# Attention's outputs turned by VectorE in 32x32 squares instead of by TensorE, with gates and results moved by squares

## What is computed

```python
h = rms_norm(x, norm_pre) * (1.0 + scale) + shift      # shift, scale, gate from silu(c) @ ada_w + ada_b
q, k, v, z = h @ w_in                                   # 4 x 2048 columns
p = softmax(mask(q k^T * scale)) for both halves m      # mask: key chunk <= query chunk
attn = p[:, :, 0] - lam * p[:, :, 1]
o = attn @ v                                            # per head, 256 wide
o = rms_norm(o, subln_g) * (1.0 - lambda_init)          # over the head's 256 values
o = o * silu(z)
x = x + gate * rms_norm(o @ w_out, norm_post)
```

## Time and profile before

| | |
|---|---|
| median of 3 runs | 1907.08 us (1906.72 to 1908.92) |
| the profiled execution | 1907.34 us |
| its span, first to last instruction | 1905.5 us |
| mean granted TensorE clock | 0.999 |

### The profile page before, as it was taken

The page is one execution under the profiler, slowest core; times in us unless marked ns, Lnnn a source line. Parts: engine busy times, 40 slices in busy tenths (PEclk is TensorE's granted clock), DMA queues, the critical chain, the costliest instruction groups (busy, mean ns, idle before and its releaser), DMA issues.

```text
span 1905.5 us, 26384 instructions
## 1 busy us (share of the span) xinstructions
PE 1866.0 (98%) x9072; PEld 1540.9 (81%) x9072; DVE 1379.5 (72%) x2028; ACT 810.1 (43%) x1516; POOL 794.4 (42%) x844
## 2 busy tenths in 40 slices
PE   4999999999999999999999999999999999999998
PEld 1488888888888888888888888888888888888886
DVE  3687888886655546787887877878778776569467
ACT  5633333333444433444443444444444445546452
POOL 2076565655644523344344434434443422116023
PEclk9999999999999999999999999999999999999999
DMA  9898898886674698786877778686777679657777
GB/s 354 253 313 279 274 297 278 284 290 232 214 267 160 237 356 263 225 250 192 253 229 227 235 216 252 198 254 212 232 240 221 213 228 291 207 186 257 258 240 265
DMA packets 394048, 473.16 MB, mean 248 GB/s; under 512 B 22614, under 2 KB 268476, under 8 KB 391228
## 3 DMA queue, kind: packets, MB, share of 16 engines
q1 hardware_dynamic: 393632, 471.43, 76.4%
q10 hardware_dynamic: 284, 0.05, 0.0%
HBM read 323.54 MB, written 147.86 MB: 247 GB/s over the span
## 4 chain that ended last, share of the span: by engine, by line
PE 93%; DVE 1%; DMA 1%; ACT 0%; issue 0%; SPq 0%; POOL 0%; DVEq 0%; POOLq 0%; ACTq 0%
PE ps L1752 30%; PE ps L1754 30%; PE ps L1753 30%; PE ps L1885 2%; PE ps L1861 1%; PE ps L1904 1%; PE ps L1721 0%; DMA ubf<-s_dr 0%; DMA z_dr<-cc 0%; PE ps L1833 0%; DVE ring L1310 0%; ACT h L1040 0%; DVE xt L1632 0%; DVE tB L1330 0%; DVE tB L1327 0%
## 5 line engine op out<-in xcount | busy, mean ns | idle before, releaser
L1752 PE MATMUL ps<-blk,ring 128*128 128x512 f32 x1524 | 603.3, 396 | 2.6 <-DVE blk L1357 1.9
L1754 PE MATMUL ps<-blk,ring 128*128 128x512 f32 x1524 | 594.6, 390 | 0.0
L1753 PE MATMUL ps<-blk,ring 128*128 128x512 f32 x1524 | 594.2, 390 | 0.0
L1752 PEld LDWEIGHTS ps<-blk,ring 128*128 128x128 f32 x1524 | 286.3, 188 | 66.0 <-issue 9.7
L1754 PEld LDWEIGHTS ps<-blk,ring 128*128 128x128 f32 x1524 | 286.0, 188 | 60.8
L1753 PEld LDWEIGHTS ps<-blk,ring 128*128 128x128 f32 x1524 | 286.5, 188 | 55.8
L1310 DVE TENSOR_TENSOR ring<-sums,ring 128x512 fp32r<-128x512 f32 x256 | 234.7, 917 | 95.5 <-ACT ring L1006 93.6
L836 POOL TENSOR_TENSOR sums<-raw 128x512 f32<-128x512 f32 x128 | 191.5, 1496 | 226.9 <-DVE ring L1310 206.0
L1006 ACT ACTIVATE ring<-sums 128x512 fp32r<-128x512 f32 x256 | 160.6, 628 | 179.3 <-PE ps L1754 175.6
L1310 DVE TENSOR_TENSOR ring<-raw,ring 128x512 fp32r<-128x512 f32 x192 | 179.2, 934 | 58.9 <-ACT ring L1006 58.5
L836 POOL TENSOR_TENSOR sums<-sums,raw 128x512 f32<-128x512 f32 x128 | 190.2, 1486 | 20.8 <-DVE ring L1310 14.3
(11 more groups left out here) (159 smaller groups left out, 3181.7 us busy)
## 6 DMA issues: line engine op xcount, KB each, us to landing
raw<-in_diff_w_in_dram SPq DMA_DIRECT2D x64, 1024.0 KB, 7.8
d_dr<-cc SPq DMA_DIRECT2D x124, 256.0 KB, 3.2
cc<-d_dr SPq DMA_DIRECT2D x124, 256.0 KB, 4.1
ubf<-s_dr SPq DMA_DIRECT2D x113, 256.0 KB, 5.0
ada<-in_ada_w_dram SPq DMA_DIRECT2D x88, 256.0 KB, 7.3
tb<-in_diff_w_out_dram SPq DMA_DIRECT2D x32, 512.0 KB, 5.5
t_dr<-tb SPq DMA_DIRECT2D x32, 512.0 KB, 4.9
ada<-in_ada_w_dram SPq DMA_DIRECT2D x32, 512.0 KB
```

The lines of the kernel that those rows point to most:

```text
L1752: MM(dst, a_hi, b_hi, start=start, stop=False, skip_group_check=True)
L1753: MM(dst, a_hi, b_lo, start=False, stop=False, skip_group_check=True)
L1754: return MM(dst, a_lo, b_hi, start=False, stop=stop, skip_group_check=True)
```

## The change

The transposition of each block's result by TensorE goes. VectorE turns the 128x256 tile within squares of 32x32 (`V.transpose`, from SBUF into the same PSUM columns); the squares themselves stay where they are. So the gate must be loaded in that arrangement of squares, and the results are stored by squares so that `s_dr` holds what it held before: each load of z and each store becomes four DMAs of 32 partitions with runs of 32 elements (128 B) in place of one DMA of 128 partitions with runs of 512 B. The norm weight, which was a value per partition after the turn, is now a row across columns (`sub_row`, one broadcast load of 128 KB, scaled once) and is multiplied in `out_scale`. `gate` becomes a transpose and one multiplication of 128x256. The layout of `s_dr` changes so that a unit's read still has 2 KB runs.

```diff
@@ load_z
-                sp.dma_start(z_sb[:, :, :],
-                             z_dr[h * 2:h * 2 + 2, :, qb * P:(qb + 1) * P].rearrange("m p n -> p m n")).then_inc(z_ld, 16)
+                for c in range(0, P, SIDE):
+                    sp.dma_start(z_sb[c:c + SIDE].rearrange("j m (b i) -> j (m b) i", i=SIDE),
+                                 z_dr[h * 2:h * 2 + 2, :, qb * P + c:qb * P + c + SIDE].rearrange(
+                                     "m (b j) i -> j (m b) i", j=SIDE)).then_inc(z_ld, 16)
@@ store_pair
                 sp.wait_ge(ozf_ok, h * NB + 2 * p + 2)
-                sp.dma_start(s_dr[0:4, h, :, p].rearrange("o p n -> p o n"),
-                             ozf.rearrange("p i m n -> p (i m) n")).then_inc(s_st, 16)
+                for c in range(0, P, SIDE):
+                    sp.dma_start(s_dr[h, 0:4 * P, p, c:c + SIDE].rearrange("(o j) i -> j o i", j=SIDE),
+                                 ozf[c:c + SIDE].rearrange("j t m (b i) -> j (t m b) i", i=SIDE)).then_inc(s_st, 16)
                 sp.wait_ge(osum_ok, 4 * (h * PAIRS + p + 1))
-                sp.dma_start(s_dr[4:8, h, :, p].rearrange("o p n -> p o n"), osum[:, :, :]).then_inc(s_st, 16)
+                for c in range(0, P, SIDE):
+                    sp.dma_start(s_dr[h, 4 * P:8 * P, p, c:c + SIDE].rearrange("(o j) i -> j o i", j=SIDE),
+                                 osum[c:c + SIDE].rearrange("j o (b i) -> j (o b) i", i=SIDE)).then_inc(s_st, 16)
@@ load_unit
-                sp.dma_start(ubf[k][:, 1, 1], s_dr[s, h].rearrange("p t n -> p (t n)")).then_inc(unit_in[k], 16)
+                sp.dma_start(ubf[k][:, 1, 1], s_dr[h, s * P:(s + 1) * P].rearrange("p t n -> p (t n)")).then_inc(unit_in[k], 16)
@@ SP, second half of the projection
+                if n == NA + 12:
+                    sp.dma_start(sub_row[:, :], subln[None, :].to_broadcast([P, VD])).then_inc(sub_in, 16)
@@ out_scale, gate (VectorE)
-                V.tensor_scalar(o_sb[:, :], ps[:, OB, 0:VD], ofac[:, 0:1], None, ALU.mult).then_inc(o_ok, 1)
+                else:
+                    dve.wait_ge(cols_ok, 2)
+                STT(o_sb[:, :], ps[:, OB, 0:VD], ofac[:, 0:1], sub_row[:, :], ALU.mult, ALU.mult).then_inc(o_ok, 1)
@@
+                dve.wait_ge(o_ok, a + 1)
+                V.transpose(ps[:, OB, VD:2 * VD], o_sb[:, :]).then_inc(oT_done, 1)
+                dve.wait_ge(z_ld, (a + 1) * 16 * (P // SIDE))
+                if a > 1:
+                    dve.wait_ge(s_st, PAIR_STORED * (a // 2))
                 dve.wait_ge(oT_done, a + 1)
-                dve.wait_ge(z_ld, (a + 1) * 16)
-                if a > 1:
-                    dve.wait_ge(s_st, 32 * (a // 2))
-                for m in range(2):
-                    i = STT(ozf[:, a % 2, m], ps[:, OB, VD + m * P:VD + (m + 1) * P], sub8[:, m:m + 1],
-                            z_sb[:, m], ALU.mult, ALU.mult)
-                i.then_inc(ozf_ok, 1)
+                TTV(ozf[:, a % 2], ps[:, OB, VD:2 * VD].rearrange("p (m n) -> p m n", m=2), z_sb[:, :, :],
+                    ALU.mult).then_inc(ozf_ok, 1)
@@ VectorE, once
+            dve.wait_ge(sub_in, 16)
+            V.tensor_scalar(sub_row[:, :], sub_row[:, :], (1.0 - LAMBDA_INIT) / 2, None, ALU.mult).then_inc(cols_ok, 1)
@@ TensorE (and its three calls)
-            def o_turn(h, qb):
-                a = h * NB + qb
-                pe.wait_ge(o_ok, a + 1)
-                for m in range(2):
-                    last = TR(ps[:, OB, VD + m * P:VD + (m + 1) * P], o_sb[:, m * P:(m + 1) * P], ident[:, :])
-                last.then_inc(oT_done, 1)
```

More of the change, by code:

```diff
@@ L16 @@
 CHUNK = 64
+SIDE = 32
 def build(nc, x, c, ada_w, ada_b, norm_pre, norm_post, w_in, w_out, lq1, lk1, lq2, lk2, subln, out):
@@ L150, in build @@
         gpT = at("gpT", [P, P], F32)
-        sub8 = at("sub8", [P, 2], F32)
         lamp = at("lamp", [P, 2], F32)
@@ L232, in build @@
         ofac = at("ofac", [P, 1], F32, z_at)
+        sub_row = at("sub_row", [P, VD], F32, z_at)
         BLK = 2 * KB * HALF * 4
@@ L267, in build @@
         t_dr = dram("t_dr", [2, HEADS, 4, P, HALF])
-        s_dr = dram("s_dr", [8, HEADS, P, PAIRS, P])
+        s_dr = dram("s_dr", [HEADS, 8 * P, PAIRS, P])
         gp_dr = dram("gp_dr", [KT, P])
@@ L280, in build @@
         lam_p, lam_mm, lam_e, lam_ok = sem("lam_p"), sem("lam_mm"), sem("lam_e"), sem("lam_ok")
-        c_e, c_ok = sem("c_e"), sem("c_ok")
+        c_ok, sub_in = sem("c_ok"), sem("sub_in")
         x_sq, x_ss, x_ms, x_rs, x_sc = sem("x_sq"), sem("x_ss"), sem("x_ms"), sem("x_rs"), sem("x_sc")
@@ L370, in turned @@
             return a // NB * (NB + HT) + qb + max(qb - HT, 0) + half + 1
+        PAIR_STORED = 2 * 16 * (P // SIDE)
         def taken(s):
@@ L713, in load_unit @@
                     s, h = {P1: 0, P2: 1, P4: 3, P5: 4, P6: 5, P7: 6, P3: 7}[op], u
-                sp.wait_ge(s_st, 32 * PAIRS * (h + 1))
-                sp.dma_start(ubf[k][:, 1, 1], s_dr[s, h].rearrange("p t n -> p (t n)")).then_inc(unit_in[k], 16)
+                sp.wait_ge(s_st, PAIR_STORED * PAIRS * (h + 1))
+                sp.dma_start(ubf[k][:, 1, 1], s_dr[h, s * P:(s + 1) * P].rearrange("p t n -> p (t n)")).then_inc(unit_in[k], 16)
             for n in range(NA, NA + PARTS_IN * NP):
+                if n == NA + 12:
+                    sp.dma_start(sub_row[:, :], subln[None, :].to_broadcast([P, VD])).then_inc(sub_in, 16)
                 if n == NA + 26:
@@ L1009, in _ @@
             act.wait_ge(c_in, 16)
-            A(cexp[:, :], craw[:, :], ACT.Exp, scale=-1.0).then_inc(c_e, 1)
+            A(cexp[:, :], craw[:, :], ACT.Exp, scale=-1.0).then_inc(c_ok, 1)
             for t in range(TT):
@@ L1282, in _ @@
             V.memset(yss[:, :, :, :], D * EPS).then_inc(yss_c, 1)
-            dve.wait_ge(c_e, 1)
+            dve.wait_ge(c_ok, 2)
             V.tensor_scalar(cexp[:, :], cexp[:, :], 1.0, None, ALU.add).then_inc(c_ok, 1)
-            dve.wait_ge(c_ok, 2)
+            dve.wait_ge(c_ok, 3)
             V.reciprocal(cexp[:, :], cexp[:, :]).then_inc(c_ok, 1)
-            dve.wait_ge(c_ok, 3)
+            dve.wait_ge(c_ok, 4)
             TTV(cact[:, :], craw[:, :], cexp[:, :], ALU.mult).then_inc(c_ok, 1)
@@ L1294, in _ @@
             TTV(lamp[:, 1:2], cols[:, R_LAM + 2:R_LAM + 3], cols[:, R_LAM + 3:R_LAM + 4], ALU.mult).then_inc(lam_p, 1)
-            V.tensor_scalar(sub8[:, :], cols[:, R_SUB:R_SUB + 2], (1.0 - LAMBDA_INIT) / 2, None, ALU.mult).then_inc(cols_ok, 1)
             dve.wait_ge(lam_e, 1)
@@ L1727, in ada_rows @@
                 if s == 0:
-                    pe.wait_ge(c_ok, 4)
+                    pe.wait_ge(c_ok, 5)
                 pe.wait_ge(*ada_landed(s))
@@ L1898, in weighted @@
                 last.then_inc(pv_done, 1)
-            def o_turn(h, qb):
-                a = h * NB + qb
-                pe.wait_ge(o_ok, a + 1)
-                for m in range(2):
-                    last = TR(ps[:, OB, VD + m * P:VD + (m + 1) * P], o_sb[:, m * P:(m + 1) * P], ident[:, :])
-                last.then_inc(oT_done, 1)
-            def before(a):
-                return divmod(a - 1, NB)
             for n in range(NA, NA + PARTS_IN * NP):
@@ L1921, in _ @@
                         n += 1
-                    if a:
-                        o_turn(*before(a))
                     cut = 1 if qb == HT - 1 else 0
@@ L1972, in _ @@
                     scores(LH, qb, 1)
-                o_turn(*((LH, qb - 1) if qb else (LH - 1, NB - 1)))
                 for i in range(n1):
@@ L1982, in _ @@
             tick(u + 1)
-            o_turn(LH, NB - 1)
             for v in range(u + 2, BEGIN[LAST]):
```

## The result

The changed kernel takes 1951.35 us, median of 4 runs (1950.71 to 1955.94), against 1907.3 us for the kernel before beside it: ratio 1.0235, 95% interval 1.0217 to 1.0252. The direction was forecast, with a chance of only 0.51, the size was not: +4 to +5 us expected, +44 measured, outside the range.

The account below looks back on a forecast made before the run. TensorE, busy 98% of the span, was taken as the bound; 1907.34 - 14.1 + 13.5 + 0.5 + 2.9 + 2.1 = 1912.2, given as 1912.0 us. Range 1897 to 1933, likeliest case 1905 to 1919.

Parts of the forecast that it names:

- -14.1 us: TensorE: two transposes per block go, 0.22 us for each of 64 blocks, all counted as time won.
- short waits ahead of the transposes: TensorE's short waits ahead of some removed transposes would go as well; left out of the sum.
- The 0.2 that it costs at qb 3: Longer gate (+0.3 us) against 0.1 margin before `weighted` at qb 3: 0.2 us in each of 7 heads.
- SP's nine issues: Nine more DMA issues per pair of blocks make qb 3's reload 1.9 us late: +13.5 us over seven heads.
- issue price of 0.52: SP's time per DMA issue in a row, bounds 0.40 to 0.54; nine make +4.7 us.
- q and k at qb 1: Later issue of k, 3.6 us at qb 1, meets more margin: +0.5 us for seven heads (0 to 3).
- The packets: 128 B runs cost an estimated 8 ns per packet, 1.6 us of queue per pair; 0 in the interleaved stage.
- The last head's start: Output unit waits for its load behind 1.6 us of issues and about 1 of queue: +2.9 us (1.6 to 4).
- the end of attention: Unit waits for the last `osum` landing, later by three issues and the longer gate: +2.1 us (1.2 to 4).
- Rival 1: SP's idle time covers more, with issues every 0.40 us: 1902 us (1894 to 1905), chance 0.25.
- Rival 2: Small packets fill the DMA queues, 128 B taking as long as 512 B: 1928 us (1919 to 1940), chance 0.18.
- Rival 3: Each small write takes two passes, holding gates another 5 us in every pair: above 1945 us, chance 0.05.

Follow-up runs that it names:

- whole transfers: Changed kernel, but z loaded and each store written by one DMA of 128 partitions with 512 B runs, squares not put in place: 1900.5 us, ratio 0.9959.
- packets alone: Changed kernel, but one DMA of 128 partitions per z load and store, still with 128 B runs, data not where they belong: 1910.46 us, ratio 1.0012.
- issues alone: Changed kernel with its four DMAs of 32 partitions per z load and store, but 512 B runs, squares not put in place: 1939.37 us, ratio 1.0166.

## Why the prediction was wrong

**The bound and the transposes.** TensorE was the bound, as read, and each pair of transposes takes 0.22 us of it. But "-14.1 us" was too much: with nothing else in the way 7 came through. The step that failed is the remark that short waits ahead of the transposes would go as well. The transposes were themselves the cover of a `prob` with less than 0.2 us of margin, at three of eight blocks: 4.0 us of the 7.1 that are missing. The other 3.1 are at `weighted`, behind the longer gate.

**VectorE.** The turn takes 0.45 us and the multiplication 0.43 (0.42 and 0.42 forecast), `out_scale` 0.48 as before. Right. The 0.2 that it costs at qb 3 was less than half of what the run with whole transfers shows: 3.1 us in seven heads in place of 1.4.

**SP's nine issues.** Place, chain and count are as forecast: the reload at qb 3, seven heads, `take`, gate, `aT_low`, `weighted`. Two terms failed. The first is the issue price of 0.52 with bounds 0.40 to 0.54. It came from a few issues of one block; twelve in a row took 0.52 to 0.72 each, and one took 2.7 us (z's load at 915.61 took 4.24 us for four, right behind a load of 1 MB). Of z's parts (count, ns min/median/max):

```profile
L569 SPq DMA_DIRECT2D z_sb<-z_dr x256: 303/451/2721, 791.3 to 1720.3; - x128
```

In the second head the reload was 4.9 us late in place of 1.9, and in all there were stands of 33.2 us in place of 11.9. Since most of SP's cover was used up by then, each tenth more per issue went straight through: 9 x 0.15 is more than 1 us in each head. Second, a stand was priced at its own length. The work at half clock that came with it was no term at all, and it is 10 to 18 us.

**q and k at qb 1** were forecast at 0.5 (0 to 3); the row "issue" has 5.3 us, 4.7 of it in six of the heads. There k went out 3.7 to 5.3 us later against TensorE's need than before, where 3.6 had been forecast: the same error in the issue price.

**The packets** were put at 0 in the interleaved stage. Alone they cost 10.0 us, most of it by the late reload behind longer issues, a way that the forecast did not have.

**The last head's start and the end of attention.** From the first matmul of `weighted` at block 56 to that at block 63 it is 116.7 us against 114.4, so with 1.5 of transposes gone some 3.9 were lost, where 2.9 had been forecast (with whole transfers the stretch takes 111.5, by which 5.2 were lost). TensorE waited 3.2 us of it for `prob` and not for the unit alone. For the end of attention "+2.1" did not come: from there to the end of the span 225.8 against 226.0 us.

```profile
1744.01 1.93 SPq L581 DMA_DIRECT2D s_dr<-osum  x4
...
1747.43 0.34 SPq L723 DMA_DIRECT2D ubf<-s_dr  x1
...
1752.93 1.06 ACT L1187 ACTIVATE ub<-ubf 128x1024 fp32r<-128x1024 f32 x1 [1.13 <-DMA ubf<-s_dr]
```

From the first of the four issues to the unit's load it is 3.4 us, and in before 3.1, from the single issue at 1695.44 to the row of 1698.54. Issuing four takes 1.6 us more, but the small transfers land while the next are being issued, and only the last one's short landing counts. All transfers of `s_dr` in the changed kernel, stores and the units' loads (the stores alone have a median of 2.0 and 5.5 at most):

```profile
DMA to landing us min/median/max: 1.8/2.1/9.3
```
I had added three issues to an unchanged landing.

**The account.** From the span with whole transfers (1897.3 - 1905.5 = -8.2): waits for `aT_low` 33.2 - 1.7, for q and k 5.3, for `prob` 3.5 - 1.3, clock 16.6 in the heads. Sum +47.4, against +48.6 measured. It is a sum over one execution; the medians lie 4.6 us lower.

**The rivals.** Rival 1 (1902) fell: the idle time covered less, not more. Rival 2 (1928) had the right sign, but its mechanism fell by its own mark, landings of stores at 6 us or more: none took that long, no gate waited for them, and packets alone make 10 us. Rival 3 (above 1945) had the number with a chance of 0.05, but not the cause: a packet of 128 B took 13.1 ns and not longer than a whole one. None had a second price behind the wait, and the range ended 18 us too low.

The Trainium skill ("DMA: Bandwidth & Descriptors", Rules for kernel authors) says of two transfers to disjoint halves of the partitions that they aren't worth it, as both use the same DMA engines, and advises one of 128 partitions. The run with issues alone, which has quarters, agrees in sign, with 38.9 us; the cost that the trace shows for it lies in the issuing queue.

Open: why an issue in a row takes up to 0.72 and not 0.52. How busy the DMA engines are does not explain it: twelve issues took 0.67 each at 76% and 0.62 each at 54% (904.22 to 911.68), and before's took 0.36 to 0.50 at 98%. With runs of 512 B (issues alone) they took 0.47 to 0.63, so the small pieces are a part of it. A gate placed behind `aT_low`, which would have hidden VectorE's part, was not tried: the turn and `weighted` use the same PSUM bank.

## What to carry over

An engine that issues DMAs has a budget like any other: sum its busy and idle time ahead of each load that is due soon, price issues in a row at the worst that the trace shows and not at one block's (single issues of up to 1.5 us stood in the trace of before), and look at the order in the queue first, since a load moved ahead of stores gave back nearly everything here. Price a stand of TensorE of some microseconds as the stand plus a stretch of work at half clock. And an operation taken off the bounding engine gains only what the next operand's margin leaves; read that margin at every block before multiplying by their number.

## What the runs showed of the hardware

- Around stands of TensorE its granted clock was 0.5 for 3.41 or 6.83 us; in the changed kernel five of six such stretches began before the stand ended. There the stands of 5.0, 5.4, 5.6, 5.6 and 6.4 us (start to start) came with 6.83 us, that of 4.6 with 3.41, those of 3.3 and 2.6 with nothing; with the stores alone in squares, three of five stands of 2.0 to 2.8 us were followed by 3.41. All 13 stands of over 4 us from the first head's attention on, in all runs of this case, had one of the two. At 2 to 4 us it came in some cases and not in others, and the runs don't tell which. With unused matmuls in the stand the clock stayed at 1.00; with the same matmuls behind a stand of 2.8 to 4.2 us it fell in six of seven heads.
- One HBM transfer split into four by partitions costs the issuing engine 0.30 us per part at least and 0.45 to 0.51 on the median. Twelve such issues in a row took 0.52 to 0.72 each, and a single one behind a load of 1 MB 2.7. Three groups of four issues by ScalarE (z's, in the second head) took 1.8 to 2.6 us, 0.45 to 0.66 each.
- A packet of 128 B takes 13.1 ns of its DMA engine on the mean and one of 512 B 28.4, by the changed kernel's trace. Small pieces also make the issue longer: 1.18 us against 0.36 for 256 KB.
- VectorE turns 128x256 f32 in squares of 32x32 from SBUF into PSUM in 449 ns.
